# Transposes by DMA, a convolution half in three pieces, and another selection rule in a bidirectional GLA and short-convolution block

## What is computed

```
u = rms_norm(h, g_pre)
proj = jnp.einsum('bld,dn->bln', u, w_in)
(c_b, c_c, c_x, c_z, q, k, v, r, lr_f, lr_b, m_a, m_b) = jnp.split(proj, split_idx, axis=-1)

y_conv = c_b * short_conv_centred(c_c * c_x, conv_w) * jax.nn.silu(c_z)
p_conv = jnp.einsum('blc,cd->bld', y_conv, w_out_c)

o_f = gla_chunked(qc, kc, vc, gfc, strict=False)         # j <= t
o_b = rev(gla_chunked(rev(qc), rev(kc), rev(vc), rev(gbc), strict=True))  # j > t
o = rms_norm(o, gla_g).reshape(bn, L, DV)                # per-head group norm
y_gla = o * jax.nn.silu(r)
p_gla = jnp.einsum('blc,cd->bld', y_gla, w_out_g)

merged = jax.nn.sigmoid(m_a) * p_conv + jax.nn.sigmoid(m_b) * p_gla
out = jnp.einsum('bld,de->ble', merged, w_out)
return h + rms_norm(out, g_post)
```

## Time and profile before

| what | value |
|---|---|
| median of 3 runs | 3026.55 us (3025.92 to 3027.06) |
| profiled execution, own time | 3030.86 us |
| its span, slowest core (core 4) | 3029.3 us |
| spans of the eight cores | 3013.9 to 3029.3 us |
| granted TensorE clock | 0.987 to 0.992 of full speed |
| TensorE, busy share of the span | 96% |
| DVE, ACT, POOL | 67%, 55%, 33% |

### The profile page before, as it was taken

One profiled execution on the slowest core, in us unless ns is written; L12 is line 12 of the kernel. 1 busy time (PEld: TensorE's weight loads), 2 busy tenths in 40 slices (PEclk: granted clock), 3 DMA queues, 4 the chain that ended last, 5 costly groups with the idle time before them and its releaser, 6 DMA issues.

```text
span 3029.3 us, 56330 instructions; the slowest of 8 cores (3013.9 to 3029.3 us)
## 1 busy us (share of the span) xinstructions
PE 2895.9 (96%) x17212; PEld 1522.4 (50%) x17212; DVE 2031.4 (67%) x3109; ACT 1679.7 (55%) x3171; POOL 998.4 (33%) x1387
## 2 busy tenths in 40 slices
PE   5999899899999999999999999999999999999998
PEld 3555554344456655444445665444445555544443
DVE  5767587666767667676576767757667666766665
ACT  5777664334666775442457776444356777544243
POOL 4455564332412224142232223324223222422222
PEclk9999999999999999999999999999999999999999
DMA  6666666754531112474451111347354111144545
GB/s 177 148 149 153 136 153 189 218 183 139 160 102 48 45 39 69 151 223 136 147 176 59 44 41 43 105 140 243 123 174 128 52 41 38 44 138 147 145 134 165
DMA packets 166436, 374.70 MB, mean 124 GB/s; under 512 B 16112, under 2 KB 47728, under 8 KB 165632
## 3 DMA queue, kind: packets, MB, share of 16 engines
q1 hardware_dynamic: 157216, 354.13, 37.7%
q0 software_dynamic: 8928, 16.98, 4.0%
HBM read 324.52 MB, written 65.60 MB: 129 GB/s over the span
## 4 chain that ended last, share of the span: by engine, by line
PE 84%; DVE 4%; issue 4%; DMA 3%; ACT 2%; POOL 2%; SPq 0%; DVEq 0%; POOLq 0%; ACTq 0%
PE ps L473 81%; PE ps L478 2%; DMA sb_W<-wst 1%; DMA sb_onT<-x 1%; ACT L490 1%; DMA sb_ycT<-x 1%; DVE sb_GR L499 1%; DVE sb_TB L503 1%; POOL sb_stat L676 0%; DMA wst<-sb_OS 0%; DVE sb_CS L503 0%; DVE sb_ycT L499 0%; DMA wsc<-sb_W 0%; POOL sb_CS L499 0%; ACT sb_AT L490 0%
## 5 line engine op out<-in xcount | busy, mean ns | idle before, releaser
L473 PE MATMUL ps<-sb_uT,sb_W 128*128 128x512 bf16 (+2 forms) x7680 | 1610.0, 367 | 5.0 <-ACT sb_CS L490 1.5
L473 PEld LDWEIGHTS ps<-sb_uT,sb_W 128*128 128x128 bf16 (+1 forms) x7680 | 691.3, 98 | 785.1 <-issue 33.8
L490 ACT ACTIVATE sb_CS<-ps 128x512 f32<-128x512 f32 x448 | 265.8, 594 | 370.1 <-PE ps L473 357.0
L473 PE MATMUL ps<-sb_GR 128*128 128x512 bf16 (+2 forms) x1792 | 350.2, 319 | 14.0 <-DVE sb_ycT L503 7.2
L499 POOL TENSOR_TENSOR sb_GR<-sb_CS 128x512 bf16<-128x512 f32 x128 | 166.8, 1305 | 590.4 <-DVE sb_CS L503 582.6
L473 PE MATMUL ps<-sb_GR,sb_W 128*128 128x512 bf16 x1072 | 263.7, 380 | 11.4 <-ACT sb_LR L490 7.9
L503 DVE SCALAR_TENSOR_TENSOR sb_CS<-sb_CS,sb_convw 128x512 f32<-128x512 bf16 x256 | 222.3, 878 | 42.9 <-ACT sb_CS L490 29.1
L499 DVE TENSOR_TENSOR sb_CS<-ps,sb_CS 128x512 bf16<-128x512 f32 (+1 forms) x256 | 176.1, 688 | 108.4 <-PE ps L473 80.6
L473 PE MATMUL ps<-sb_W,sb_uT 128*128 128x256 bf16 x2048 | 241.6, 275 | 7.1 <-DVE sb_ycT L499 5.9
L473 PEld LDWEIGHTS ps<-sb_GR 128*128 128x128 bf16 x1792 | 163.9, 98 | 146.0 <-issue 16.8
L499 POOL TENSOR_TENSOR sb_CS<-sb_CS 128x512 f32<-128x512 f32 x128 | 166.0, 1299 | 172.7 <-DVE sb_CS L503 146.8
(11 more groups left out here) (165 smaller groups left out, 4225.5 us busy)
## 6 DMA issues: line engine op xcount, KB each, us to landing
sb_W<-wsc SPq DMA_DIRECT2D x272, 256.0 KB, 2.9
sb_W<-wst SPq DMA_DIRECT2D x128, 512.0 KB, 4.2
sb_W<-wst SPq DMA_DIRECT2D x128, 384.0 KB, 3.3
sb_onT<-x SPq DMA_DIRECT2D x50, 512.0 KB, 7.7
sb_GR<-x SPq DMA_DIRECT2D x40, 512.0 KB, 5.9
sb_OS<-w_pairs SPq DMA_DIRECT2D x32, 512.0 KB, 5.0
y<-sb_GR SPq DMA_DIRECT2D x32, 512.0 KB, 3.0
sb_ycT<-x SPq DMA_DIRECT2D x32, 512.0 KB, 6.1
```

The lines of the kernel that those rows point to most:

```text
L473: S.add("pe", lambda e: e.matmul(out, lhsT=lhsT, rhs=rhs, start=start, stop=stop, skip_group_check=skip), r, w, cost=max(0.025, free_n(rhs ...
L490: S.add("act", lambda e: e.activation(out=out, in_=in_, func=func, **kw), r, w, table=TABLE.get(func), cost=0.17 + 0.82e-3 * free_n(in_) + ...
```

## The change

Four edits.

1. **Transposes by DMA.** A new helper `dtr` issues a transposing DMA on SP. It takes over `f_tr` (128 KB each), `b_T` (64 KB), the blocks of `b_T2` (as a new step `b_X`, 128 KB, into one buffer `oX`), and `s0_tr` (256 KB), except for the first eight token tiles of the first sequence. `b_M` now multiplies by `gla_norm` too (an operand of 256 columns instead of a column), and `b_T2` is one multiplication of `oX` into `onT`. The new steps have chains of their own (`FX`, `BX`, `OX`) and conditions: `f_tr` waits for the last reader of `KTf`, `b_T` for the products of u - 2, `b_X` for the `b_T2` of u - 1, and `b_O` for the `b_X` of u - 2.
2. **First convolution half in three pieces** of 342, 342 and 341 tokens, which hold token 1024; `halo` goes (in the first sequence 8 matmuls for the meta token stay, in the last piece's bank).
3. **Another selection rule** in `cost` and `run`, and a higher modelled DMA rate; a transposing DMA holds SP for 1.1 in the model.
4. GpSimd's DMA scratch is halved; `glag` becomes a 128x256 constant.

```diff
-        e, r, t = starts[0]
-        return max(0.0, r - max(t, now), (t - now - (BACKLOG if it.lim is None else it.lim)) if e != "sp" else 0.0)
+            over = [after[e] - after["pe"] - FULL for e in ("act", "dve", "pool") if after[e] > before[e]]
+            return True, sum(pe), CROWD * sum(max(0.0, o) for o in over)
...
+        late = (r - now) if r > t else 0.0
+        return False, max(late, (t - now - (BACKLOG if it.lim is None else it.lim)) if e != "sp" else 0.0, 0.0), 0.0
...
-                if best is None or w < best[0] - 1e-9:
-                    best = (w, c, it)
-                if w <= TOL:
+                is_pe, w, crowd = x
+                if w + crowd <= TOL:
+                    pick = (w, c, it)
                     break
...
+            if pick is None:
+                pick = side if side and (pe is None or side[0] <= wait) else pe
...
+        def dtr(out, in_, r, w, semkey, nbytes):
+            S.add("sp", lambda e: e.dma_start(out=out, in_=in_, transpose=True), r, w, semkey=semkey, nbytes=nbytes, hold=1.1)
...
-        def s0_tr(us, i):
+        def s0_tr(us, i, b):
             u_ap, u_k = us
+            if b or i >= 8:
+                dst = REG["uT"][:, :].rearrange("p (k t) -> p k t", k=8)[:, :, i * 128:(i + 1) * 128]
+                keys = [g for k in range(8) for g in uT[k](BF16, i * 128, 128)[1]]
+                dtr(dst, u_ap, u_k, keys, ("xt", u_k[0]), 1 << 18)
+                return
...
         def f_tr(H, g):
-            tb, tbk = npsb()
-            for z in range(4):
-                s_ap, s_k = H.kin(0, (g * 4 + z) * 128, 128)
-                tr(tb[:, z * 128:(z + 1) * 128], s_ap, s_k, tbk)
+            s_ap, s_k = H.kin(0, g * 512, 512)
             o_ap, o_k = KTf(BF16)
-            evac(o_ap, tb[:, 0:512], tbk, o_k)
+            dtr(o_ap.rearrange("p (c t) -> p c t", t=128), s_ap, s_k, o_k, ("ktf",), 1 << 17)
...
+        def b_X(u):
+            s_ap, s_k = ON[u % 2](BF16)
+            o_ap, o_k = oX(BF16)
+            dtr(o_ap.rearrange("p (c t) -> p c t", t=128), s_ap, s_k, o_k, ("ox",), 1 << 17)
...
-            def halo(h):
...
+            cuts = [(0, 512), (512, 512)] if hh else [(0, 342), (342, 342), (684, 341)]
...
-                            put("F2", lambda H=H, g=g: f_tr(H, g), None, [("km",) + me + (0,)])
+                            put("FX", lambda H=H, g=g: f_tr(H, g), ("ft",) + me + (g,),
+                                [("km",) + me + (0,)] + ([("P",) + me + (1,)] if g else [("P",) + pm + (3,)] if has_prev else []))
```

More of the change, by code:

```diff
@@ L86, in __init__, with add @@
         self.starts = None
-    def add(self, eng, fn, reads=(), writes=(), semkey=None, extra=(), cost=0.1, table=None, nbytes=0):
+    def add(self, eng, fn, reads=(), writes=(), semkey=None, extra=(), cost=0.1, table=None, nbytes=0, hold=0.06):
         op = Op(eng, fn, semkey)
@@ L276, in cost @@
         now = S.free["pe"]
+        before = dict(S.free)
         try:
@@ L279, in cost @@
             starts = S.starts
+            after = dict(S.free)
         except NotReady:
@@ L297, in run @@
         while left:
-            best = None
+            pe = side = pick = None
+            wait = 0.0
             for c in self.order:
@@ L324 @@
 BACKLOG = 3.0
+FULL = 4.0
+CROWD = 0.1
 IDLE = 2.0
@@ L628, in program @@
         e1 = Buf("AT", 4 * KB, 8 * KB)
[L629 to L632, removed]
+        ccb = [[Buf("CS", i * 1536, 1536) for i in range(3)], [Buf("CS", i * 2048, 2048) for i in range(2)]]
+        pvb = [Buf("CS", 4608 + i * 2304, 2304) for i in range(2)]
+        tcb = [Buf("CS", 9216 + i * 2048, 2048) for i in range(2)]
+        szb = [Buf("CS", 13312 + i * 1024, 1024) for i in range(2)]
         p7junk = Buf("TB", 0, 2048)
@@ L1066, in conv_units, with piece @@
             me = (b, hh, j)
-            def halo(h):
+            cuts = [(0, 512), (512, 512)] if hh else [(0, 342), (342, 342), (684, 341)]
+            last = len(cuts) - 1
+            def piece(n, s):
+                a, w = cuts[s]
                 bank, bk = nps()
-                wb = wbuf(h)
-                for k in range(8):
-                    w_ap, wkk = wb(BF16, k * 128, 128)
-                    u_ap, uk = uT[k](BF16, 1024, 1)
-                    mm(bank[:, 0:1], w_ap, u_ap, k == 0, k == 7, wkk + uk, bk)
-                if b == 0:
+                proj(hs[n], 0, 128, t0 + a, w, bank, bk)
+                if b == 0 and hh == 0 and s == last:
+                    wb = wbuf(hs[n])
                     for k in range(8):
@@ L1151, in cb @@
                     rel(hs["cb"])
-            put("C", edges, None, [("cx", me, 1)])
+            put("C", edges, None, [("cx", me, last)])
             for s in range(2):
@@ L1159, in conv_units @@
                 put("C", lambda s=s: zmul(s), ("zm", me, s), [("z", me, s)])
-            edge = [("ST", b, 8)] if hh == 0 else []
-            return ([(lambda s=s: cc(s), None, edge if s else []) for s in range(2)] +
-                    [(lambda s=s: cx(s), ("cx", me, s), edge if s else []) for s in range(2)],
+            edge = lambda s: ([("ST", b, 8)] if s == last and hh == 0 else []) + ([("M0", 2)] if b == 0 else [])
+            return ([(lambda s=s: cc(s), None, edge(s)) for s in range(last + 1)] +
+                    [(lambda s=s: cx(s), ("cx", me, s), edge(s)) for s in range(last + 1)],
                     [(lambda s=s: z(s), ("z", me, s), []) for s in range(2)],
```

129 lines of the change are left out of this document (59 added, 70 removed).

## The result

The changed kernel takes 2982.4 us (median of 4 runs, 2979.6 to 2984.0) where the kernel before takes 3026.2 beside it (3024.4 to 3027.1): a ratio of 0.9855, 95% interval 0.9838 to 0.9872. The forecast was 2950 with a range of 2905 to 3015, so the sign and the range held, and 32 us of the forecast gain are missing. The profiled execution of the changed kernel took 2982.3 us, its span is 2980.7. In some executions the cores of one die, or of both, show a lower granted clock and take longer; the times and ratios here are those of the other executions.

What follows compares the result with a forecast made beforehand. TensorE's issue was taken to bound the kernel; -82 - 12 - 8 + 8 + 12 + 5 = -77 from 3030.9 gave 2954 us profiled, so 2950 us for the runs, range 2905 to 3015.

Steps and rivals of the forecast that it cites:

- What bounds the kernel: Whole kernel: TensorE, busy 96% of the span, bounds by what it must issue; little can come from waits.
- Start, +5: First sequence: its second eight token tiles pass the DMA queue at its busiest, +5 us, ends 0 and 20.
- Transposes, -82: Token tiles, decayed keys, head values: 1472 transposes leave TensorE at 56 ns each, -82 us, all on the path.
- thirds, -12: First convolution half in three pieces: 64 units fall from 3656 to 3460 ns, -12 us.
- Forward keys, +8: Refills of the single buffer `KTf`: TensorE waits for each DMA to land, taken as L = 3.5 us, +8 us.
- Head values to stage 6, +12: Start of stage 6: last head-value transposes queue behind the 2 MB load, +4 us in each of three later sequences.
- The transposes' own waits, -8: TensorE: the transposes' waits for `sb_AT` and `sb_ON`, 4.4 and 3.3 us, go, -8 us.
- The rule, 0: Planner's selection rule: only permutes TensorE's work, taken as 0, ends -30 and +30 us.
- The engines: Expected busy times: TensorE lower by 90 to 150 us, ACT by about 100, DVE by about 70.
- The queue is not full: Rival, SP's queue: 376 transposing DMAs fill it and weights come late, 3060 us, slower than before; chance 0.16.
- Landing at 6 us: Rival, `KTf` refills: transposing DMAs land after 6 us, refills cost 49 us instead of 8, 2991 us; chance 0.13.
- The signs: Changed profile: 15,740 TensorE instructions, `sb_KT` waits under 10 us; wrong if landing reaches 6 us or queue share passes 60%.

Runs made afterwards that it cites:

- experiment 3: Changed kernel with the first sequence's token tiles 8 to 15 transposed on TensorE again: 2953 us, ratio 0.9705; with all its transposes back: 2946.3 us.
- experiment 7: Changed kernel with forward keys moved in pairs, two buffers of two blocks instead of one of four: ratio 0.9869 to the kernel before.
- experiment 5: Kernel before with the new cost and selection rule alone: ratio 0.9983; changed kernel with the old ones put back: ratio 1.0291.

## Why the prediction was right, and where it was not

**What bounds the kernel.** "TensorE runs without a gap there, so all of it is on the path": this is the step that failed, for a quarter of the work. It holds in the later sequences (62 us forecast and measured). In the first, 43 us of idle time stood in the earlier trace rows and 11.3 us of waits for `wst` in the earlier trace rows; I added them up as small instead of asking which wait ends last there. Already in the kernel before the chain of preparations set that sequence's end: the thirds alone gave it nothing. For the first sequence the sum should have had only the 8 us that came off behind the chain's end, not -18 less 3.

**Start, +5.** The cost was seen in the right place, and priced at the wrong one. The first landmark did not come later; but the token transposes held back `r` and with it the first `w_pairs` load. That load stands 19.4 us later than in the kernel before, and 33 us later than in the changed kernel with its token tiles on TensorE (93.8 against 60.6 us, experiment 3). The chain's end followed by 21.4 us, where the term had 5. With the point above (21 us counted, 8 had) this makes the 29 us between forecast and traces.

**Transposes, -82, thirds, -12.** Right in price. Three later sequences by 384 blocks by 56 ns are 64.5 us, and with the other terms the measured 62 come out. Pieces of 342 columns start 146 ns apart, as priced:

```profile
1563.14 1.32 PE L488 MATMUL ps<-sb_uT,sb_W 128*128 128x342 bf16 x8
1564.31 0.38 PE L488 MATMUL ps<-sb_GR,sb_KT 128*128 128x256 bf16 x2
```

**Forward keys, +8.** 29.5 us: mis-sized by 21. I took L = 3.5 us with 0.6 for SP. The landing alone was shorter in the median, 2.5 (the 192 of `sb_KT` are 64 of forward keys, 128 KB each, and 128 of backward keys, 64 KB each; all 192 are shown as one):

```profile
sb_KT<-sb_GR SPq DMA_TRANSPOSE x192, 2.5
...
sb_OX<-sb_ON SPq DMA_TRANSPOSE x128, 2.5
...
sb_uT<-sb_ycX SPq DMA_TRANSPOSE x28, 4.9
sb_uT<-sb_AT SPq DMA_TRANSPOSE x24, 5.0
```

SP's part was up to 5, behind another transpose that waits (experiment 7). The gap in TensorE's order at the worst place is the 1.8 us that I had counted; the other gaps hid what they should. Each later sequence so lost 6 to 7 us instead of 1.7. The estimate from the Trainium skill ("VectorE: DVE Perf Modes", section "The three transpose paths"), 5.2 us for four blocks, is not what the trace shows. The Trainium skill also says that transposing DMAs are as fast as regular ones ("Advanced Engine Details and Errata", section "X-Bar Transpose (TRN2)"). The 128 KB of head values agree, 2.5 us beside 2.7 for 128 KB of `smeta` in the same trace. For the 256 KB of tokens the trace leaves it open: 4.9 and 5.0 beside 2.9 for `wsc` weights, but the fastest of them landed after 3.0, and in the first sequence the keys, too, took up to 11.1.

**Head values to stage 6, +12.** About 1: the waits for `sb_onT` are 1.4 us in all, none for `sb_OS` by DMA. The least of 26 us that I estimated against 23 to 25 was too high: in the second sequence DVE had written these sums by 1219.1, 22.6 us after the loop's last product started (1196.5). This and the keys cancel in each later sequence, so that the right sum there rests in part on two errors of 4 us.

**The transposes' own waits, -8.** They are gone, as said; the waits for `sb_AT` and `sb_ON` that are left (4.6 and 3.4 us, by ACT) belong to other steps.

**The rule, 0.** Right by itself (experiment 5), wrong as a term of this sum: the -82 are only to be had with it. A planner's rule that is neutral for one kernel decides, for another, whether new latencies are covered; here it did.

**The engines.** TensorE's busy time fell by 80 us where I had 90 to 150. More of its work now runs at 1.2 GHz; an estimate of what that adds is 593 us by 0.98 less 0.94, or some 24 us, which would account for the difference to my range; ACT's fell by 104 as said, DVE's by 16 instead of 70: its products into `onT` fell from 111.7 to 70.3 us as counted, but the planner handed it work that several engines can do (70 multiplications into `sb_SB` instead of 12, 44.1 us instead of 4.5).

**The rivals.** The queue is not full: q1's share is 47.9%, so the 376 transposing DMAs added some 286 us to its 1142, 0.8 us each and not 4.8. Landing at 6 us did not happen. The measured time lies in that rival's band, 2976 to 3015; its mechanism (refills) gives 21 of its 41 us. So it is partly luck that the range held: the forecast's own 2925 to 2975 does not contain 2982, the range went further for a rival that did not come about, and what filled it was the chain, which no term had.

**The signs.** TensorE's 15,740 instructions and the 342 columns came as said, and none of the four signs of being wrong was seen (landing taken by its medians). The waits on `sb_KT`, named at under 10 us, are 29.5. I took the stretches of 757 us for sequences; by landmarks a later one took 730 to 733 us.

## What to carry to other kernels

Ask for every stretch which chain ends last before pricing the engine that is busiest over the whole: where a side chain bounds, columns saved on TensorE turn into waits, and a delay at the chain's head can come out nearly whole at its end (22 us of start gave 21 of end here; the rule alone moved the start by 17 and the end by 2). A DMA that replaces engine work is priced by its place on its queue, by what waits ahead of it, more than by its landing; halving its size did not help here. Price a change of the order together with the operations it is made for, not by itself.

## What the hardware showed that was not expected

A transposing DMA held SP's queue 1.18 us for its issue, where plain ones held it 0.3 to 0.6 (one in 0.32, two in 0.93, five in 2.80); the packets of that queue more than doubled, from 157,216 to 357,664, for 14% more bytes, and its share rose from 37.7% to 47.9%.

A wait of TensorE cost more than its length: behind the waits of 14.3 and 9.0 us the matmuls ran at 1.2 GHz for a while, with starts 420 ns apart instead of 216, and the granted clock of the first sequence's stretch was 0.94 instead of 0.98.
